# Router, row turning and clears of a conv/GLA + mixture-of-experts step rebuilt, one wait moved, fillers dropped

## The chip, the cores and the metric

One NeuronCore of a Trainium2 chip runs the whole program. The metric is the device time of one launch in microseconds; lower is better. The engines are TensorE (PE, products; PEld its weight loads), VectorE (DVE), ScalarE (ACT), GpSimd (POOL) and SyncE (SP, which only issues the loads).

## The reference

320 tokens (256 of a prompt, 64 of a running stream) of width 1024 go through two layers in fp32:

```python
for l in range(2):
    m = mixer(x, ...)                    # short gated convolution and gated linear attention, one in and one out projection
    x = layer_norm(ALPHA * x + m)
    if l == 0: f = (silu(x @ w_gate) * (x @ w_up)) @ w_down          # 1024 -> 3584 -> 1024
    else:
        logits = x @ router                                          # 8 experts
        top_v, top_i = top_k(logits, 2); gates = softmax(top_v)
        f = sum over the token's two experts of gate * swiglu_e(x)
    x = layer_norm(ALPHA * x + f)
```

## The kernel before

**Layout.** x lies transposed in SBUF: 8 column blocks of 128 model columns by 320 tokens (x[:, k, :]). Each fp32 product with weights is made of three fast ones: both operands are split into a rounded part and a rest (xh, xl; whi, wlo), and hi*hi, lo*hi and hi*lo are added up in PSUM. Weights arrive in units of 1 MB in a ring of six (raw); ACT rounds a unit (round_unit), DVE forms its rest (rest_unit), both two units ahead of PE (ring of three). SP loads unit n when the rest of unit n-6 exists (load). Units 0 to 15 are layer 0's mixer, 16 to 57 the dense mixer (7 chunks of 6), 58 to 73 layer 1's mixer, from 74 the experts. Every engine runs its program in the order written; semaphores tie them together.

**A norm** (norm on each engine) runs over the model columns, thus over partitions. DVE adds each new x[k] into rstd and each of ACT's squares into sq_sum while the blocks come; PE multiplies the sums by a matrix of 1/1024 (mean_d) and so spreads mean and mean square over all partitions (ps[4], ps[5]). DVE forms the variance (L1417, L1420), ACT Ln and Exp (L1096, L1098), DVE centres (L1423) and scales (L1441) each block; ACT adds the bias. Where the norm is split (behind layer 0's mixer and behind the dense mixer), ACT writes xh (L1102), DVE writes xl (L1432) and POOL adds the bias to x itself (add_bias, L550). PE fills its waits with products that nobody reads (keep_busy, L642; the counts stand in BUSY).

**The end of the dense mixer** (dense_mixer, last chunk): PE's unit 57 gives x[4] to x[7]; DVE adds each block to x (L1673), then into the sums; ACT rounds units 58 and 59, loads the table set for Ln and Exp (L1230) and then squares (L1088). DVE's rest of unit 59 stands behind its last addition. PE waits for the fourth addition and then does 8 fillers.

**Layer 1's mixer** begins with two_tiles over unit 58 block by block as xl comes, then 16 low-rank products (L792, L793) behind a wait for all of POOL's x, then unit 59.

**The router** stands behind layer 1's first norm, whose last step on ACT is x itself (L1107). PE multiplies x[k], as the weights loaded, by the 8 router columns, for three tiles of tokens (t): 24 fp32 products (L876), each two instructions. Then 24 transposes turn x into rows of tokens (L885), in six halves (512 columns each) in XT_ORDER. ACT rounds each half (xt_hi, L1247), DVE forms its rest (xt_lo, L1709). DVE clears lg, does rest_unit(76) and six memsets (clear), copies the logits (L1730) and ranks them (L1736 to L1743), marks first and second (sel1, sel2, sel) and forms the difference for the gates; each such small operation waits for the one before (step). PE counts places in each expert's list (L891 to L895), does 14 fillers and then four gathers (L914): the products of the turned rows with a 0/1 matrix (pick, L1832), which put the tokens of the first two experts side by side. ACT and DVE split what comes (xg). Before the first two gathers ACT must have kept two turned halves (kept, L1240), which frees their banks.

**The experts.** A pair of experts takes 84 units; pair() steps through gate and up units, transposes of the hidden rows (T, L977) and down units. In the first pair DVE also does the tables of the routing. hm is silu(gate)*up (L1901).

Of the kernel before, what the change touches and what calls it, by code (L numbers as in the profile page):

```python
# [33 lines left out]
def hybrid_stream_step(nc, x_prompt, x_sample, cache_conv, state_gla, ln_mix_g, ln_mix_b, w_in, w_alpha2,  # L34
# [86 lines left out]
    with ctx:  # L121
# [13 lines left out]
        mean_v = sb("mean_v", [P, P])  # L135
# [13 lines left out]
        w_rt = sb("w_rt", [P, KT, E])  # L149
# [255 lines left out]
        def _(sp):  # L405
# [16 lines left out]
            def parameters():  # L422
# [14 lines left out]
                sp.dma_start(w_rt[:], moe_router[0].rearrange("(k p) e -> p k e", p=P)).then_inc(small_landed, 16)  # L437
# [65 lines left out]
        def _(pool):  # L503
# [13 lines left out]
            const(pool.memset(mean_v[:], 1.0 / DV))  # L517
# [88 lines left out]
        def _(pe):  # L606
# [1409 lines left out]
```

## Time and profile before

| | us |
|---|---|
| median of 3 runs (lowest, highest) | 1613.78 (1612.58, 1614.01) |
| the profiled execution's own time | 1612.82 |
| its span | 1611.2 |
| PE busy | 1584.7 (98%) |
| DVE busy | 1248.0 (77%) |
| ACT busy | 1023.9 (64%) |
| POOL busy | 36.2 (2%) |
| granted TensorE clock, mean | 0.993 |

The span runs from the first to the last instruction that the profile holds; the time of a run is a little longer. A busy share is an average over stages with different limits. An fp32 product is two instructions of PE in the profile, an fp32 transpose one, and their ends are modelled, so distances between starts say more than durations. A granted clock of 1 is 2.4 GHz, of 0.5 it is 1.2 GHz.

### The profile page before, as it was taken

Reading aid. Unit: us, or ns where it says so; the run is one execution under the profiler, and the core shown is the slowest. Engines: PE = TensorE matmul, PEld = TensorE weight load, DVE = VectorE, ACT = ScalarE, POOL = GpSimd, SP = SyncE. Lnnn points to the kernel's source line nnn. Section 1 sums busy time; section 2 is a strip of 40 time slices with the busy share of each in tenths; the row PEclk is TensorE's granted clock in tenths of the full one; section 3 lists DMA queues with packets and bytes.
Section 4 is the critical chain, followed back from the end, with each engine's and each line's share of the span. In section 5 each row is a group of like instructions: output and inputs, shape, how many; then the busy total and the mean of one; then the engine's idle time right before and its main releaser. Section 6 shows DMA issues by size and latency. Waiting matters only on the chain.

```text
span 1611.2 us, 23720 instructions
## 1 busy us (share of the span) xinstructions
PE 1584.7 (98%) x8698; PEld 1405.7 (87%) x8698; DVE 1248.0 (77%) x1420; ACT 1023.9 (64%) x1178; POOL 36.2 (2%) x67
## 2 busy tenths in 40 slices
PE   9999999999989999999999999999999999999997
PEld 8998999999989998888888888888888888888885
DVE  5577554544475677999998998988898988898996
ACT  4454333333344555878777877877877877877875
POOL 1002000000010000000000000000000001000100
PEclk9999999999999998999999999999999999999999
DMA  9524644444424342999998999998999999999992
GB/s 300 165 79 161 214 155 156 143 143 156 144 92 131 106 138 102 364 374 372 383 380 330 383 370 380 385 370 324 381 371 375 384 377 351 385 395 378 387 394 80
DMA packets 226208, 445.41 MB, mean 276 GB/s; under 512 B 10498, under 2 KB 72656, under 8 KB 226064
## 3 DMA queue, kind: packets, MB, share of 16 engines
q1 hardware_dynamic: 223920, 434.16, 74.9%
q0 software_dynamic: 2192, 9.98, 1.7%
q8 instruction: 59, 0.97, 0.2%
q14 instruction: 37, 0.30, 0.1%
HBM read 438.59 MB, written 8.67 MB: 278 GB/s over the span
## 4 chain that ended last, share of the span: by engine, by line
PE 93%; DVE 4%; ACT 1%; issue 1%; DMA 0%; DVEq 0%; ACTq 0%
PE ps L964 18%; PE ps L939 13%; PE ps L941 13%; PE ps L940 13%; PE ps L610 10%; PE ps L611 10%; PE ps L612 10%; PE ps L977 1%; PE ps L914 1%; DVE x L1441 1%; DVE x L1423 1%; PE ps L642 0%; DVE wlo L1356 0%; DVE xl L1432 0%; PE ps L1009 0%
## 5 line engine op out<-in xcount | busy, mean ns | idle before, releaser
L1356 DVE TENSOR_TENSOR wlo<-raw,whi 128x1024 fp32r<-128x1024 f32 x672 | 778.2, 1218 | 48.8 <-ACT whi L1063 47.5
L1063 ACT ACTIVATE whi<-raw 128x1024 fp32r<-128x1024 f32 x672 | 677.3, 1055 | 59.7 <-PE ps L964 54.1
L939 PE MATMUL ps<-whi,xg 128*128 128x512 f32 x896 | 353.9, 395 | 0.0
L941 PE MATMUL ps<-whi,xg 128*128 128x512 f32 x896 | 349.5, 390 | 0.0
L940 PE MATMUL ps<-wlo,xg 128*128 128x512 f32 x896 | 348.9, 389 | 0.0
L1351 DVE TENSOR_TENSOR wlo<-raw,whi 128x2048 fp32r<-128x2048 f32 x73 | 167.5, 2294 | 128.2 <-ACT whi L1059 128.2
L610 PE MATMUL ps<-xh,whi 128*128 128x320 f32 x832 | 259.8, 312 | 4.7 <-DVE xl L1432 4.4
L612 PE MATMUL ps<-xh,wlo 128*128 128x320 f32 x832 | 257.1, 309 | 0.0
L611 PE MATMUL ps<-xl,whi 128*128 128x320 f32 x832 | 257.0, 309 | 0.0
L941 PEld LDWEIGHTS ps<-whi,xg 128*128 128x128 f32 x896 | 168.2, 188 | 35.8
L940 PEld LDWEIGHTS ps<-wlo,xg 128*128 128x128 f32 x896 | 168.4, 188 | 33.6
L939 PEld LDWEIGHTS ps<-whi,xg 128*128 128x128 f32 x896 | 168.3, 188 | 33.4
L1059 ACT ACTIVATE whi<-raw 128x2048 fp32r<-128x2048 f32 x73 | 139.1, 1906 | 62.9 <-PE ps L612 60.4
L610 PEld LDWEIGHTS ps<-xh,whi 128*128 128x128 f32 x832 | 156.1, 188 | 9.2 <-issue 4.5
L611 PEld LDWEIGHTS ps<-xl,whi 128*128 128x128 f32 x832 | 156.2, 188 | 0.2
L612 PEld LDWEIGHTS ps<-xh,wlo 128*128 128x128 f32 x832 | 156.2, 188 | 0.0
L964 PE MATMUL ps<-whi,hT_hi 128*128 128x512 f32 x440 | 135.6, 389 | 0.0
L964 PE MATMUL ps<-wlo,hT_hi 128*128 128x512 f32 x440 | 135.5, 389 | 0.0
L964 PE MATMUL ps<-whi,hT_lo 128*128 128x512 f32 x440 | 135.5, 389 | 0.0
L1305 ACT ACTIVATE hT_hi<-ps 128x512 fp32r<-128x512 f32 x56 | 33.6, 599 | 101.4 <-PE ps L977 101.0
L964 PEld LDWEIGHTS ps<-whi,hT_lo 128*128 128x128 f32 x440 | 82.6, 188 | 17.2
L964 PEld LDWEIGHTS ps<-wlo,hT_hi 128*128 128x128 f32 x440 | 82.6, 188 | 17.2
(322 smaller groups left out, 1506.4 us busy)
## 6 DMA issues: line engine op xcount, KB each, us to landing
raw<-in_moe_w_gate SPq DMA_DIRECT2D x112, 1024.0 KB, 8.1
raw<-in_moe_w_up SPq DMA_DIRECT2D x112, 1024.0 KB, 8.2
raw<-in_moe_w_down SPq DMA_DIRECT2D x112, 1024.0 KB, 7.6
raw<-in_w_in SPq DMA_DIRECT2D x23, 1024.0 KB, 5.5
raw<-in_ffn_w_gate SPq DMA_DIRECT2D x14, 1024.0 KB, 5.0
raw<-in_ffn_w_up SPq DMA_DIRECT2D x14, 1024.0 KB, 5.0
raw<-in_ffn_w_down SPq DMA_DIRECT2D x14, 1024.0 KB, 5.0
raw<-in_w_out SPq DMA_DIRECT2D x8, 1024.0 KB, 5.2
```

Of the source, the lines that this page charges most:

```text
L610: pe.matmul(out, wh, hi, start=start and j == 0, stop=False)
L611: pe.matmul(out, wh, lo, start=False, stop=False)
L612: mm = pe.matmul(out, wl, hi, start=False, stop=stop and j == len(pairs) - 1)
L939: pe.matmul(bank[:], xh_k, wh, start=k == 0, stop=False)
L940: pe.matmul(bank[:], xh_k, wl, start=False, stop=False)
L941: mm = pe.matmul(bank[:], xl_k, wh, start=False, stop=k == KT - 1)
L964: mm = pe.matmul(ps[4 + d][:], hT[:, c % 2, k, :], slot(w, n, SPLIT, 2)[:, j, 512 * d:512 * d + 512], start=fc == 0 and k == 0 and hT is h ...
L1059: act.activation(flat(whi, n, SPLIT), flat(raw, n, RAW), ACT.Copy).then_inc(hi_ready, 2)
L1063: act.activation(part(whi, n, SPLIT, h), part(raw, n, RAW, h), ACT.Copy).then_inc(hi_ready, 1)
L1305: act.activation(hT_hi[:, c % 2, :, :].rearrange("p f s -> p (f s)"), bank[:], ACT.Copy).then_inc(hT_hi_ready, 1)
L1351: dve.tensor_tensor(flat(wlo, n, SPLIT), flat(raw, n, RAW), flat(whi, n, SPLIT).bitcast(F32), ALU.subtract).then_inc(lo_ready, 2)
L1356: dve.tensor_tensor(part(wlo, n, SPLIT, h), part(raw, n, RAW, h), part(whi, n, SPLIT, h).bitcast(F32), ALU.subtract).then_inc(lo_ready, 1)
```

## The change

1. **Logits.** The router weights get 120 zero columns behind them (w_wide), a slice of 128 columns from 8k on is the loaded operand, and x[:, k, :] (320 columns) moves: 8 products into ps[0], of whose rows the first 8 are read. DVE copies them (lgT), PE turns them with three small transposes, DVE copies the result into lg. Behind these transposes PE does 9 fillers, and 5 instead of 14 ahead of the first gather.
2. **Turned rows.** The three transposes of block k follow the logit product of block k (the last two blocks behind all logits). XT_ORDER is now the first halves of all three token tiles, then the second halves, in other banks; ACT rounds the first three halves inside the norm, between its last blocks of x. The first two gathers wait for the first three rests alone.
3. **Selection.** sel is one comparison (rank below 2) and one memset. sel1, sel2, the gates' difference and the table copy stand behind the four gathers on DVE, and ACT's Exp of the difference behind its last kept half. The first pick reads qpos itself.
4. **Clears.** Five memsets go to POOL, which waits for the last unit of layer 1's mixer, and PE waits for them before the gathers; gT is cleared only in its last 64 columns. acc_sum stays with DVE.
5. **Units.** rest_unit(76) goes to the end of DVE's router. Unit 59 is rounded on ACT behind the Exp of the norm behind the dense mixer and its rest is formed behind that norm on DVE. The table load stands behind the fourth square.
6. **Waits and fillers.** In layer 1 PE no longer waits for POOL's x ahead of the low-rank products; DVE waits for it, block by block, where it updates x at the mixer's end. The 8 fillers behind the dense mixer are dropped.
7. mean_v (1/128) is dropped: the products use ones, and ACT's Ln gets the scale 1/128.

```diff
@@ -146,7 +145,8 @@
         w_a2 = sb("w_a2", [LRC, DEPTH, HEADS * DK])
-        w_rt = sb("w_rt", [P, KT, E])
+        w_wide = sb("w_wide", [P, KT * E + P - E])
+        w_rt = w_wide[:, 0:KT * E].rearrange("p (k e) -> p k e", e=E)
         u_mem = sb("u_mem", [P, CT * (T + 2 * (CONV_W - 1))])
@@ -371,9 +373,10 @@
-        BUSY = {"x lands": 5, "x tile": 2, "first unit": 5, "norm": 19, "last chunk": 8, "first gather": 14}
-        RT_LOGITS, RT_SEL, RT_DIFF = 4, 14, 19
-        XT_ORDER = [1, 2, 3, 4, 5, 0]
+        BUSY = {"x lands": 5, "x tile": 2, "first unit": 5, "norm": 19, "logits": 9, "first gather": 5}
+        RT_LOGITS, RT_SEL, RT_DIFF = 2, 11, 23
+        XT_ORDER = [0, 2, 4, 1, 3, 5]
+        XT_BANK = {0: 6, 2: 7, 4: 3, 1: 4, 3: 5, 5: 2}
         SMALL_LOADS = 4
@@ -571,6 +574,13 @@
         add_bias(1, o_ffn_b, 1.0)
+pool.wait_ge(unit_used, 2 * (U_OUT[1] + UNITS_OUT))
+for n, rows_of in enumerate((xt_hi[TOK[2]:P, 2, :].bitcast(F32), xt_lo[TOK[2]:P, 2, :].bitcast(F32),
+                             acc[TOK[2]:P, 2, :], gT_hi[:, T:TT * P].bitcast(F32),
+                             gT_lo[:, T:TT * P].bitcast(F32))):
+    if n:
+        pool.wait_ge(cleared, n)
+    pool.memset(rows_of, 0.0).then_inc(cleared, 1)
 pool.wait_ge(y_parked, 16)
...
     idle = ps[0 if stage == 3 else 7]
-    if stage == 1:
-        pe.wait_ge(d_added, 8 * FC + KT // 2)
-        keep_busy(BUSY["last chunk"], idle)
     pe.wait_ge(summed, (KT - 1) * (stage + 1))
@@ -783,8 +790,8 @@
-    pe.wait_ge(x_ready, KT * (1 + 2 * l))
     if l == 0:
+        pe.wait_ge(x_ready, KT)
         pe.wait_ge(small_landed, 16 * SMALL_LOADS)
@@ -869,22 +876,28 @@
+def turn_rows(k):
+    for t in range(TT):
+        mm = pe.transpose(ps[XT_BANK[2 * t + k // 4]][0:TOK[t], P * (k % 4):P * (k % 4) + P],
+                          x[:, k, P * t:P * t + TOK[t]], ident[:])
+        if k % 4 == 3:
+            mm.then_inc(xt_done, 1)
+
 def router():
...
         pe.wait_ge(x_ready, 3 * KT + k + 1)
-        for t in range(TT):
-            mm = pe.matmul(ps[t][0:TOK[t], 0:E], x[:, k, P * t:P * t + TOK[t]],
-                           w_rt[:, k, :], start=k == 0, stop=k == KT - 1)
+        mm = pe.matmul(ps[0][:, 0:T], w_wide[:, E * k:E * k + P], x[:, k, :], start=k == 0, stop=k == KT - 1)
+        if k < KT - 2:
+            turn_rows(k)
     mm.then_inc(lg_done, 1)
-
-    for j in XT_ORDER:
-        t, half = j // 2, j % 2
-        if j == 0:
-            pe.wait_ge(rt_step, RT_LOGITS)
-        for k in range(4):
-            mm = pe.transpose(ps[2 + j][0:TOK[t], P * k:P * k + P],
-                              x[:, 4 * half + k, P * t:P * t + TOK[t]], ident[:])
-        mm.then_inc(xt_done, 1)
+    turn_rows(KT - 2)
+    turn_rows(KT - 1)
+
+    pe.wait_ge(rt_step, RT_LOGITS)
+    for t in range(TT):
+        mm = pe.transpose(ps[1][0:TOK[t], E * t:E * t + E], lgT[:, P * t:P * t + TOK[t]], ident[0:E, 0:E])
+    mm.then_inc(lg_turned, 1)
+    keep_busy(BUSY["logits"], ps[0])
@@ -896,9 +909,10 @@
     keep_busy(BUSY["first gather"], ps[0])
-    pe.wait_ge(xtl_ready, 2 * TT)
+    pe.wait_ge(cleared, 5)
     pe.wait_ge(pick_ready, 1)
     for g in range(GATHERS):
+        pe.wait_ge(xtl_ready, TT if g < 2 else 2 * TT)
         if g < 2:
@@ -1081,6 +1095,13 @@
+def turned_hi(n):
+    j = XT_ORDER[n]
+    t, half = j // 2, j % 2
+    act.wait_ge(xt_done, n + 1)
+    act.activation(xt_hi[0:TOK[t], t, 512 * half:512 * half + 512], ps[XT_BANK[j]][0:TOK[t], :], ACT.Copy
+                   ).then_inc(xth_ready, 1)
+
 def square(stage, k):
...
     act.activation(rstd[:], rstd[:], ACT.Exp, scale=-0.5).then_inc(rstd_ready, 1)
+    if stage == 1:
+        round_unit(U_IN[1] + 1)
     if split:
...
                        ).then_inc(x_ready, 1)
+        if k >= KT - TT:
+            turned_hi(k - (KT - TT))
@@ -1226,38 +1252,36 @@
         chunk(c)
-    chunk(FC - 1)
-    act.preload_act_table_set(LOG_EXP)
+    chunk(FC - 1, last=True)
     for k in range(KT):
...
         square(1, k)
+        if k == 3:
+            act.preload_act_table_set(LOG_EXP)
     norm(1, o_ffn_b, True)
...
 def router():
-    def kept(j):
+    def kept(n):
+        j = XT_ORDER[n]
         t, half = j // 2, j % 2
-        act.wait_ge(xtl_ready, XT_ORDER.index(j) + 1)
-        act.activation(acc[0:TOK[t], t, 512 * half:512 * half + 512], ps[2 + j][0:TOK[t], :], ACT.Copy,
+        act.wait_ge(xtl_ready, n + 1)
+        act.activation(acc[0:TOK[t], t, 512 * half:512 * half + 512], ps[XT_BANK[j]][0:TOK[t], :], ACT.Copy,
                        scale=ALPHA).then_inc(acc_ready, 1)
...
+    for n in range(TT, 2 * TT):
+        turned_hi(n)
     round_unit(U_MOE + AHEAD)
-    for n, j in enumerate(XT_ORDER):
-        t, half = j // 2, j % 2
-        act.wait_ge(xt_done, n + 1)
-        act.activation(xt_hi[0:TOK[t], t, 512 * half:512 * half + 512], ps[2 + j][0:TOK[t], :],
-                       ACT.Copy).then_inc(xth_ready, 1)
-    act.wait_ge(rt_step, RT_DIFF)
-    act.activation(top[:, 3, :], top[:, 2, :], ACT.Exp).then_inc(rt_exp, 1)
-
-    kept(4)
-    kept(5)
+    kept(0)
+    kept(1)
     for g in range(GATHERS):
...
         if g == 1:
-            kept(1)
-    for j in (2, 3, 0):
-        kept(j)
+            kept(2)
+    for n in range(3, 2 * TT):
+        kept(n)
+    act.wait_ge(rt_step, RT_DIFF)
+    act.activation(top[:, 3, :], top[:, 2, :], ACT.Exp).then_inc(rt_exp, 1)
     act.preload_act_table(ACT.Silu)
@@ -1631,6 +1655,8 @@
                 dve.wait_ge(tile_done, TD_OUT[l] + u + 1)
+            if l:
+                dve.wait_ge(x_ready, 2 * KT + m + 1)
             dve.scalar_tensor_tensor(out=x[:, m, :], in0=x[:, m, :], scalar=ALPHA, in1=ps[m % 4][:, 0:T],
@@ -1677,24 +1703,13 @@
                             add_to_squares(1, k - 1)
-        if last:
-            rest_unit(U_IN[1] + 1)
...
     norm(1, o_ffn_g, o_ffn_b, True)
-
-def clear():
-    dve.wait_ge(unit_used, 2 * (U_OUT[1] + UNITS_OUT))
-
-    dve.memset(xt_hi[TOK[2]:P, 2, :].bitcast(F32), 0.0)
-    dve.memset(xt_lo[TOK[2]:P, 2, :].bitcast(F32), 0.0)
-    dve.memset(acc[TOK[2]:P, 2, :], 0.0)
-    dve.memset(acc_sum[:], 0.0)
-    dve.memset(gT_hi[:].bitcast(F32), 0.0)
-    dve.memset(gT_lo[:].bitcast(F32), 0.0).then_inc(m_hid, 1)
+    rest_unit(U_IN[1] + 1)
@@ -1722,13 +1737,14 @@
     dve.wait_ge(stored, 16 * LAYER_STORES * DEPTH)
+    dve.memset(acc_sum[:], 0.0).then_inc(m_hid, 1)
     step(dve.memset(lg[:], 0.0))
-    rest_unit(U_MOE + AHEAD)
-    clear()
     dve.wait_ge(lg_done, 1)
-    for t in range(TT):
-        step(dve.tensor_copy(lg[0:TOK[t], t, :], ps[t][0:TOK[t], 0:E]))
+    step(dve.tensor_copy(lgT, ps[0][0:E, 0:T]))
     assert n == RT_LOGITS
+    dve.wait_ge(lg_turned, 1)
+    step(dve.tensor_copy(lg[:, 0:2, :], ps[1][:, 0:2 * E].rearrange("p (t e) -> p t e", e=E)))
+    step(dve.tensor_copy(lg[0:TOK[2], 2, :], ps[1][0:TOK[2], 2 * E:3 * E]))
@@ -1741,28 +1757,31 @@
     step(dve.tensor_reduce(rank[:], cmp_gt[:], AXX, ALU.add))
+    step(dve.tensor_scalar(sel[:], rank[:], 2.0, None, ALU.is_lt))
+    dve.memset(sel[TOK[2]:P, 2, :], 0.0).then_inc(rt_step, 1)
+    n += 1
+    assert n == RT_SEL
+
+    xt_rest(0, TT)
+    dve.wait_ge(pos_done, 1)
+    step(dve.scalar_tensor_tensor(out=qpos[:], in0=ps[1][:, 0:TT * E].rearrange("p (t e) -> p t e", e=E),
+                                  scalar=1.0, in1=sel[:], op0=ALU.add, op1=ALU.mult))
+    make_pick(0, qpos)
+    xt_rest(TT, 2 * TT)
+    step(dve.tensor_copy(over_n[:, 0:E], ps[1][:, TT * E:TT * E + E]))
+    for g in range(GATHERS):
+        read_gather(g)
+    step(dve.tensor_copy(q_tab[:, :, 0:STATIC], qpos[:, :, 0:STATIC]))
     step(dve.tensor_scalar(sel1[:], rank[:], 0.0, None, ALU.is_equal))
...
     step(dve.memset(sel2[TOK[2]:P, 2, :], 0.0))
-    step(dve.tensor_tensor(sel[:], sel1[:], sel2[:], ALU.add))
-    assert n == RT_SEL
-
-    for m, s in enumerate((sel1, sel2)):
-        step(dve.tensor_tensor(tmp_e[:], s[:], lg[:], ALU.mult))
+    for m, sel_m in enumerate((sel1, sel2)):
+        step(dve.tensor_tensor(tmp_e[:], sel_m[:], lg[:], ALU.mult))
         step(dve.tensor_reduce(top[:, m, :], tmp_e[:], AXX, ALU.add))
...
     assert n == RT_DIFF
-    xt_rest(0, 4)
-    dve.wait_ge(pos_done, 1)
-    step(dve.scalar_tensor_tensor(out=qpos[:], in0=ps[1][:, 0:TT * E].rearrange("p (t e) -> p t e", e=E),
-                                  scalar=1.0, in1=sel[:], op0=ALU.add, op1=ALU.mult))
-    step(dve.tensor_copy(q_tab[:, :, 0:STATIC], qpos[:, :, 0:STATIC]))
-    make_pick(0)
-    xt_rest(4, 2 * TT)
-    step(dve.tensor_copy(over_n[:, 0:E], ps[1][:, TT * E:TT * E + E]))
-    for g in range(GATHERS):
-        read_gather(g)
+    rest_unit(U_MOE + AHEAD)
     return step
```

## Rows read from the trace of the kernel before

**Rows 1.** The page, chain of work that ended last, shares of the span by engine.
```profile
PE 93%; DVE 4%; ACT 1%; issue 1%; DMA 0%; DVEq 0%; ACTq 0%
```

**Rows 2.** Timeline, PE, end of the dense mixer (start, us, engine, line, operation, count).
```profile
448.51 1.95 PE L642 MATMUL ps<-mean_d 128*128 128x128 f32 x16
```

**Rows 3.** Timeline, DVE, same stretch (in brackets: idle before it, and its releaser).
```profile
445.48 0.33 DVE L1412 COPY u_mem<-u_mem 128x320 f32<-128x320 f32 x1 [3.90 <-ACT u_mem L1088]
...
452.35 0.48 DVE L1673 TENSOR_TENSOR x<-x,ps 128x320 f32<-128x320 f32 x1
...
455.47 0.48 DVE L1417 SCALAR_TENSOR_TENSOR u_mem<-u_mem,ps 128x320 f32<-128x320 f32 x1
```

**Rows 4.** Timeline, ACT, same stretch.
```profile
441.75 1.91 ACT L1059 ACTIVATE whi<-raw 128x2048 fp32r<-128x2048 f32 x1 [4.25 <-PE ps L612]
```

**Rows 5.** Busy time by stretch: width, PE, PEld, DVE, ACT, POOL, granted clock, DMA share, GB/s.
```profile
600.90:611.30 10.40, 10.40 (x51) 9.71 (x52) 7.98 (x17) 6.23 (x10) 0.00 (x0) 0.51 0.31 101
...
614.50:621.40 6.90, 6.90 (x35) 6.90 (x35) 5.33 (x13) 1.39 (x3) 0.00 (x0) 0.52 0.01 4
```

**Rows 6.** Timeline, DVE, router.
```profile
604.00 2.36 DVE L1356 TENSOR_TENSOR wlo<-raw,whi 128x1024 fp32r<-128x1024 f32 x2 [1.61 <-ACT whi L1063]
...
610.53 0.50 DVE L1730 COPY lg<-ps 128x8 f32<-128x8 f32 x3
...
613.02 0.18 DVE L1744 TENSOR_SCALAR sel<-rank 128x24 f32<-128x24 f32 x1
...
614.97 2.48 DVE L1709 TENSOR_TENSOR xt_lo<-ps,xt_hi 128x512 fp32r<-128x512 f32 x4
...
617.78 0.96 DVE L1832 TENSOR_TENSOR pick<-slot_no,q_tab 128x768 fp32r<-128x768 f32 x1
```

**Rows 7.** Timeline, PE, router.
```profile
598.59 1.68 PE L876 MATMUL ps<-w_rt,x 128*128 128x8 f32 x13
...
606.82 5.02 PE L885 MATMUL ps<-ident,x 128*128 128x128 f32 x24
...
613.94 0.40 PE L891 MATMUL ps<-sel,before 128*128 128x24 f32 x2 [2.10 <-DVE sel L1748]
...
615.81 6.11 PE L642 MATMUL ps<-mean_d 128*128 128x128 f32 x28
...
621.68 0.61 PE L914 MATMUL ps<-pick,xt_hi 128*128 128x256 f32 x3
...
627.82 0.40 PE L939 MATMUL ps<-whi,xg 128*128 128x512 f32 x1
```

**Rows 8.** Timeline, DVE and PE, the norm of layer 1.
```profile
592.08 0.49 DVE L1634 SCALAR_TENSOR_TENSOR x<-x,ps 128x320 f32<-128x320 f32 x1 [1.38 <-PE ps L612]
...
593.27 0.70 PE L687 MATMUL ps<-u_mem,mean_d 128*128 128x320 f32 x2
...
593.81 0.70 PE L689 MATMUL ps<-u_mem,mean_d 128*128 128x320 f32 x2
...
594.60 0.49 DVE L1417 SCALAR_TENSOR_TENSOR u_mem<-u_mem,ps 128x320 f32<-128x320 f32 x1 [1.50 <-PE ps L689]
```

**Rows 9.** Timeline, PE, first and last of 16 spacings, low-rank products of layer 1.
```profile
469.77 0.31 PE L792 MATMUL ps<-xh,w_split 128*128 128x320 f32 x1
...
472.11 0.31 PE L610 MATMUL ps<-xh,whi 128*128 128x320 f32 x1
```

**Rows 10.** Timeline, ACT, last blocks of x.
```profile
601.00 1.95 ACT L1107 ACTIVATE x<-x,prm 128x320 f32<-128x320 f32 x4 [0.30 <-DVE x L1441]
```

**Rows 11.** A line's instructions, ns min/median/max; and POOL's timeline at the start.
```profile
L1432 DVE SCALAR_TENSOR_TENSOR xl<-x,prm,xh x16: 536/542/819, 150.1 to 467.3; 128x320 fp32r<-128x320 f32 x16
...
6.49 0.52 POOL L543 MEMSET v_tok<- 64x512 f32 x1
```

**Rows 12.** Timeline, DVE and PE, first pair of experts.
```profile
639.62 0.68 DVE L1901 TENSOR_TENSOR hm<-sg,ps 128x512 f32<-128x512 f32 x1
...
641.45 0.60 PE L977 MATMUL ps<-ident,hm 128*128 128x128 f32 x4
```

More of the change, by code:

```diff
@@ L134, in hybrid_stream_step @@
         mean_d = sb("mean_d", [P, P])
-        mean_v = sb("mean_v", [P, P])
         ones = sb("ones", [P, P])
@@ L295, in hybrid_stream_step @@
         gb_rows = x[:, :, :].rearrange("p k t -> p (k t)")[:, 0:2 * D].rearrange("p (a d) -> p a d", a=2)
+        lgT = hm[0:E, 0, 0:T]
         y_park = nc.dram_tensor("y_park", [SLOTS * P, D], F32).ap()
@@ L331, in hybrid_stream_step @@
         d_silu, d_hid, d_hh, d_hl, d_added = (sem(n) for n in ("d_silu", "d_hid", "d_hh", "d_hl", "d_added"))
+        lg_turned, cleared = sem("lg_turned"), sem("cleared")
         lg_done, xt_done, xth_ready, xtl_ready, rt_step, rt_exp, pos_done, ctl_ready = (sem(n) for n in (
@@ L436, in parameters @@
                                  ).then_inc(small_landed, 16)
-                sp.dma_start(w_rt[:], moe_router[0].rearrange("(k p) e -> p k e", p=P)).then_inc(small_landed, 16)
+                sp.dma_start(w_rt, moe_router[0].rearrange("(k p) e -> p k e", p=P)).then_inc(small_landed, 16)
             def given_states():
@@ L516, in _ @@
             const(pool.memset(mean_d[:], 1.0 / D))
-            const(pool.memset(mean_v[:], 1.0 / DV))
+            const(pool.memset(w_wide[:, KT * E:], 0.0))
             const(pool.memset(ones[:], 1.0))
@@ L777, in mean_squares @@
                         pe.wait_ge(o_sq[l], h + 1)
-                        pe.matmul(ps[4 + h][:, 0:T], mean_v[:], proj[:, h, :], start=True, stop=True
+                        pe.matmul(ps[4 + h][:, 0:T], ones[:], proj[:, h, :], start=True, stop=True
                                   ).then_inc(ms_done[l], 1)
@@ L1160, in rms @@
                         act.wait_ge(ms_done[l], h + 1)
-                        act.activation(proj[:, TV + h, :], ps[4 + h][:, 0:T], ACT.Ln, bias=cst[:, 0:1]
+                        act.activation(proj[:, TV + h, :], ps[4 + h][:, 0:T], ACT.Ln, bias=cst[:, 0:1], scale=1.0 / DV
                                        ).then_inc(ms_act[l], 1)
@@ L1208, in dense_mixer, with chunk @@
             def dense_mixer():
-                def chunk(c):
+                def chunk(c, last=False):
                     for j in range(PER_CHUNK):
-                        round_unit(U_FFN + j + AHEAD, c, PER_CHUNK)
+                        if not last or j < 5:
+                            round_unit(U_FFN + j + AHEAD, c, PER_CHUNK)
                         q = j // 2
@@ L1708, in xt_rest @@
                         cols = slice(512 * half, 512 * half + 512)
-                        dve.tensor_tensor(xt_lo[0:TOK[t], t, cols], ps[2 + j][0:TOK[t], :],
+                        dve.tensor_tensor(xt_lo[0:TOK[t], t, cols], ps[XT_BANK[j]][0:TOK[t], :],
                                           xt_hi[0:TOK[t], t, cols].bitcast(F32), ALU.subtract).then_inc(xtl_ready, 1)
@@ L1826, in lo_of_pair, with make_pick @@
                                   xg[:, 2 * g:2 * g + 2, 0, :].bitcast(F32), ALU.subtract).then_inc(job_read, 1)
-            def make_pick(i):
+            def make_pick(i, tab=q_tab):
                 at = slice(2 * i, 2 * i + 2) if isinstance(i, int) else bass.ds(i * 2, 2)
@@ L1832, in make_pick @@
                 dve.tensor_tensor(pick[:], slot_no[:].unsqueeze(1).unsqueeze(1).to_broadcast(full),
-                                  q_tab[:, :, at].unsqueeze(3).to_broadcast(full), ALU.is_equal).then_inc(pick_ready, 1)
+                                  tab[:, :, at].unsqueeze(3).to_broadcast(full), ALU.is_equal).then_inc(pick_ready, 1)
             def rows_of_tokens(c, step):
```

## The prediction

> **What bounds the kernel now.** I read the chain that ended last first: TensorE (PE) holds 93% of it [rows 1]. An engine full of products gains only where its products are not the limit, so I looked next for stretches in which it sits idle, runs at half clock or multiplies fillers. The change touches two of them: the norm behind the dense mixer (about 440 to 461 us) and the router (about 595 to 628 us).
>
> In the first, the last product of the dense mixer is issued just ahead of 448.51, where eight fillers follow it at once [rows 2]; yet VectorE (DVE) adds the last column block x[7] only at 452.35 [rows 3]. The reason stands in its timeline: it waited 3.90 us, to 445.48, for the first square [rows 3], and ScalarE (ACT) was late with it because it rounded a unit of weights that is not needed yet (1.91 us, from 441.75, itself held up by PE) and then loaded a table [rows 4].
>
> In the router PE looks 100% busy, and isn't. Its granted clock is 0.51 from 600.9 to 611.3 and 0.52 from 614.5 to 621.4 [rows 5]: 1.2 in place of 2.4 GHz. What it did before the first fall was logits with 8 moving columns; before the second it was idle 2.10 us. DVE holds the sum of the waits: it forms the logits' ranks only from 610.53, because the weight rest of 604.00 (2.36 us) and six memsets stand ahead of them [rows 6]. Behind the selection PE does 14 fillers, 615.81 to 621.68, though the pick is there at 617.78 + 0.96 = 618.74 [rows 6, 7].
>
> **The norm behind the dense mixer.** With the weight unit (U_IN[1]+1) moved behind the norm on both engines and the table load behind the fourth square, ACT is free when x[0] is added. DVE then needs 1.33 us for one block (445.48 to 452.35 holds a short copy and five of them [rows 3]) and PE gives a block in 12 products of 0.146, 1.76 us (16 stand between 469.77 and 472.11 [rows 9]), so PE sets the pace. x[7] follows the last product: in the next norm DVE's last addition is 592.08, 0.20 behind PE's next instruction, so 448.51 + 0.20 = 448.71 in place of 452.35: **-3.64 us**. From there to the variance the next norm, with nothing between, takes 592.08 to 594.60 = 2.52; this one took 452.35 to 455.47 = 3.12, since the weight rest stood between [rows 3, 8]: **-0.60**. ACT now rounds that unit (1.91) between the exponential and the first rounded x. The first rounded x comes later by part of that, but DVE asks for it only after three scalings and six centrings, which begin with the exponential: I take 0, with 0.9 as the other end, what would be left after two of DVE's 0.5 us operations. The removed eight fillers cover nothing any more, for PE is idle only some tenths between its last product and the mean. Price 0. What is late next: the moved rest (2.3 to 2.5 us) now ends behind the last rest of x. PE has the last third of a block and the 16 low-rank products (2.34 us [rows 9]) to do before it needs it; slack about 1.4. Its raw buffer is freed later and so the load of the unit six further on goes out about 11 us later; PE comes to that one six units of 48 products, 42 us, on. The wait for x that PE loses had no idle in front of it, since GpSimd adds its bias right behind each rest; at its reader, DVE's update of x at the end of the mixer, it is long satisfied: 0. Sum here: **-4.2**.
>
> **Router, step by step.** (a) Logits. PE starts at 598.59 as before [rows 7]. One logit product with 320 moving columns costs what the norm's sums cost at full clock, 593.27 to 593.81 = 0.54 [rows 8]; a transpose costs 5.02/24 = 0.21 at half clock [rows 5, 7], so about 0.105 at full. Six blocks of 0.54 + 3 x 0.105 = 0.86 end at 603.7; the last two products start at 603.7 and 604.3. ACT delivers the last four x by 602.95 (four in 1.95) [rows 10]; two of the three roundings of turned rows now stand ahead of the last x, 0.5 each, so it comes at 603.95: PE is the later by a little. A product is read 0.79 behind its start (593.81 to 594.60) [rows 8]: logits are readable at 605.1. Before, 610.53.
> (b) New: a copy of 8 x 320 out of PSUM. The copy of 128 x 320 in SBUF is 0.33 [rows 3], the rest of 128 x 512 out of PSUM is 2.48/4 = 0.62 [rows 6]; I take 0.4, nearer the row of the same width. Then three small transposes with their hand-over (0.6), and two copies at 0.17 (three take 0.50 [rows 6]): 606.5.
> (c) Ranks: 610.53 to 613.02 less the three copies is 2.0, as before; then one comparison and one memset (0.35) in place of five steps (0.92, 613.02 to 613.94): selection ready at 608.8. Before, 613.94 [rows 6, 7].
> (d) Whole rows: DVE takes three rests of xt (2.48/4 = 0.61 each) instead of four, then position (0.2) and pick (0.96) without the table copy: pick ready at 608.8 + 1.83 + 0.2 + 0.96 = **611.8**. PE's position products (1.3 at full clock, 2.1 if slow) and five fillers (1.1) end at 611.2 under it. The first gathers need only half 0 of all rows, and that is there. First gather at 611.9, before 621.68: **-9.8 us**.
> From there the four gathers run as before (6.14 us to the first gate product), as the three late rests of xt end at 613.7, just before the first gather can be read.
>
> **GpSimd's clears.** 64 x 512 costs 0.52 [rows 11], so three of 64 x 1024 and two of 128 x 64 cost about 3.4 us. They start behind its last stores of layer 1, beside the norm's scaling, and are wanted at 611.9. Price in itself 0. But they run beside DVE's eight operations of the norm. While GpSimd added biases, DVE's fused operation rose from 0.54 to at most 0.82 [rows 11]; eight times 0.15 is 1.2, ends 0 and 1.2. x has 0.3 in hand and PE's fillers run 0.5 over the first x, so I take **+0.3**, nearer the free end. The Trainium skill, SBUF — State Buffer, in "SBUF: two separate sides", says a DVE operation with two SBUF inputs clashes only with a GpSimd operation that reads SBUF; a memset reads nothing, and by that the term would be 0 and the sum 0.3 better.
>
> **What is queued late.** The rest of unit 76 (2.36) and 11 small steps (1.9) now stand behind the last gather on DVE, and ACT's exponential waits for those steps. With G the first gate product (627.82 before [rows 7]): steps end at G + 3.4, the rest of 76 at G + 5.8, its first half at G + 4.6; PE wants it at G + 5.5. ACT (exponential, table, one copy) starts unit 77 at G + 5.2, DVE has its first half at G + 7.5; wanted at G + 8.2. Then DVE carries the backlog: the product hm ends at G + 14.1, where it ended at G + 12.5, and PE's first transpose of it stood at G + 13.6 [rows 12]: **+0.5**. In later chunks that transpose stands behind more products. SP's load of unit 82 is released 17 us later, at G + 5.8, but it is wanted only when unit 79 is used up, about G + 17.
> The ones matrix with a scale of 1/128 in the activation, the wider router weights and one memset for another at the start change nothing on the path.
>
> **Sum.** -4.2 - 9.8 + 0.3 + 0.5 = -13.2 us. Against the profiled execution's own 1612.82 (span 1611.2) that is 1599.6; the median shown is 1.0 above it, 1613.78, so I forecast 1600.5. A measurement of this kernel can tell about 0.2%, 3.2 us, from no change.
>
> **Rivals.** *The clock falls all the same* (chance 0.2). For: between the lgT transposes and the first gather PE has pauses of some 0.6 us, small products and only 14 fillers. Against: the long stretch of 8-column products and the 2.10 us of idle are gone. In the rows it stayed at half for 6.9 us; put over positions and gathers that costs 3.4: 1603.9. The Trainium skill, TensorE: Matmul & The Clock Gate, in "Part 1: The HAM clock gate", holds that low recent activity gates the clock; the trace agrees with its 0.51, and by that rule dropping fillers is what speaks against this change.
> *The late rests hold up the first pair* (0.06). All slacks there are 0.7 to 1 us; if ACT and DVE slip by 3 us more, PE waits 3: 1603.5. Were the weight stream the limit, one lost load in advance costs the same 2.8 us.
> *The gain is taken back* (0.03): the change moves the start of the expert stage, but that stage ends by something else. Against: every load is released by DVE's rests, so the stream moves with the start. It would leave the 4.2 at most or nothing: 1610 to 1614.
> *Slower* (0.03): the gathers wait for GpSimd's five clears. DVE and GpSimd could lock each other out, each memset waiting for a gap. It decides only when the fifth ends past 611.9 + 13.2 = 625.1, that is 5.6 us a memset instead of 0.9. At 7 us each it gives 1620. Nothing in the rows is near that.
>
> **Numbers.** The forecast has 0.68 with its own range 1599 to 1602 (GpSimd 0 to 1.2, copy, hm 0 to 0.6, the rounding 0 to 0.9). The range reaches over the clock's fall and below for a better hand-over: 1597.5 to 1604.5. Faster 0.94, same 0.03, slower 0.03.
>
> **What would show it.** Right: x[7] added at about 448.7 and DVE's variance at 451.2; first product on the next weights 4.2 earlier; granted clock 1.00 from 590 through the logits; ranks begun near 602.3 (606.5 less 4.2), first gather near 607.9. Wrong: idle in front of the second input unit; a clock near 0.5 at the gathers; a wait for GpSimd's memset; idle of PE at the third or fourth unit of the first pair above 1 us.

## The result, and the profile of the changed kernel

Slower, where I had forecast 13 us faster: 1622.92 us (median of 4 runs, 1622.23 to 1623.11) against 1613.69 for the kernel before; ratio 1.006, 95% interval 1.0048 to 1.0072. The profiled execution took 1623.11, span 1621.5.

First the stretches that the change was made for. Timelines of the changed kernel, DVE and PE: the end of the dense mixer, the logits, the ranks, the first gather and the first gate product.
```profile
449.46 0.31 PE L622 MATMUL ps<-hh,wlo 128*128 128x320 f32 x1
...
449.80 0.49 DVE L1699 TENSOR_TENSOR x<-x,ps 128x320 f32<-128x320 f32 x1 [0.27 <-PE ps L622]
...
452.33 0.49 DVE L1441 SCALAR_TENSOR_TENSOR u_mem<-u_mem,ps 128x320 f32<-128x320 f32 x1 [1.51 <-PE ps L696]
...
602.01 0.48 DVE L1743 COPY hm<-ps 8x320 f32<-8x320 f32 x1 [2.74 <-PE ps L889]
...
603.36 0.36 DVE L1752 TENSOR_TENSOR cmp_gt<-lg 128x192 f32<-128x192 f32 x1
...
607.66 0.96 DVE L1851 TENSOR_TENSOR pick<-slot_no,qpos 128x768 fp32r<-128x768 f32 x1
...
608.72 0.59 PE L928 MATMUL ps<-pick,xt_hi 128*128 128x256 f32 x3 [0.32 <-issue]
...
614.89 0.40 PE L953 MATMUL ps<-whi,xg 128*128 128x512 f32 x1
```
The kernel before has that last product of the dense mixer at 448.36, just ahead of its fillers:
```profile
448.36 0.31 PE L612 MATMUL ps<-hh,wlo 128*128 128x320 f32 x1
```
It is 1.10 later here, a difference of the run's first microseconds (over all the traces, of either kernel, it scatters from 447.67 to 449.58). With it taken off, every date is the forecast one within 0.1: x[7] added at 448.70 (forecast 448.71), variance 451.23 (451.23), logits read at 600.9 (605.1 less 4.2), ranks begun 602.26 (602.3), first gather 607.6 (611.9 less 4.2). The granted clock stays up, where [rows 5] had 0.51 and 0.52 (busy time by stretch, columns as in [rows 5]):
```profile
600.00:610.00 10.00, 9.07 (x69) 7.89 (x68) 7.15 (x18) 6.00 (x10) 0.00 (x0) 1.00 0.00 0
```
The first gate product stands at 614.89, before at 627.82 [rows 7]: 12.93 us earlier, 14.03 with the start taken off. So the loss comes behind it. From the first gate product to the end of the span it took 983.4 before (1611.2 - 627.82) and 1006.6 now (1621.5 - 614.89), 23.2 more. PE waits there for 1.3 us in all in the kernel before and for 1.0 us now, so the loss is not idle time. Groups of instructions of PE, kernel before, then the changed one (busy us, mean ns | idle):
```profile
L939 PE MATMUL ps<-whi,xg 128*128 128x512 f32 x896 | 353.9, 395 | 0.0
L941 PE MATMUL ps<-whi,xg 128*128 128x512 f32 x896 | 349.5, 390 | 0.0
...
L610 PE MATMUL ps<-xh,whi 128*128 128x320 f32 x832 | 259.8, 312 | 4.7 <-DVE xl L1432 4.4 <-DVE wlo L1376 0.2
...
L964 PE MATMUL ps<-whi,hT_hi 128*128 128x512 f32 x440 | 135.6, 389 | 0.0
```
```profile
L953 PE MATMUL ps<-whi,xg 128*128 128x512 f32 x896 | 358.4, 400 | 0.0
L955 PE MATMUL ps<-whi,xg 128*128 128x512 f32 x896 | 353.8, 395 | 0.0
...
L620 PE MATMUL ps<-xh,whi 128*128 128x320 f32 x832 | 260.4, 313 | 3.9 <-DVE xl L1456 3.8
...
L978 PE MATMUL ps<-whi,hT_hi 128*128 128x512 f32 x440 | 138.3, 395 | 0.0
```
Every product with 512 moving columns is 5 to 6 ns longer; those with 320 columns are not. The same in a quiet stretch far from the change, kernel before, then the changed one: 11 products fewer in 100 us at the same clock of 1.00 and nearly the same DMA traffic (last two columns: share and GB/s).
```profile
900.00:1000.00 100.00, 100.00 (x454) 82.75 (x453) 88.98 (x83) 77.98 (x85) 0.00 (x0) 1.00 1.02 377
```
```profile
900.00:1000.00 100.00, 100.00 (x443) 80.66 (x443) 87.45 (x83) 76.66 (x84) 0.53 (x1) 1.00 1.01 369
```
The chain that ended last gives the spacing, for 24 products with the hidden rows, before and then now: 5.44 / 24 = 0.2267 and 5.60 / 24 = 0.2333 us.
```profile
650.26 5.44 PE ps L964 x24
```
```profile
637.88 5.60 PE ps L978 x24
```

The experts have 3 x 896 + 3 x 440 = 4008 such products in these groups; 23.2 us over 4008 is 5.8 ns each. That is the whole loss behind the first gate product.

### The profile page after: what moved, and what is told of

Its sections match the earlier page's. It is cut to its first block, busy times and chain, and to the rows that moved or that the text cites. A ratio compares the mean times of both kernels' runs of the same rounds, so it can differ in the third digit from the quotient of the medians.

```text
span 1621.5 us, 23644 instructions
## 1 busy us (share of the span) xinstructions
PE 1599.2 (99%) x8653; PEld 1395.3 (86%) x8653; DVE 1246.3 (77%) x1416; ACT 1022.5 (63%) x1178; POOL 43.3 (3%) x72
## 4 chain that ended last, share of the span: by engine, by line
PE 96%; DVE 3%; issue 1%; ACT 0%; DVEq 0%; POOL 0%; ACTq 0%; POOLq 0%
PE ps L978 19%; PE ps L953 13%; PE ps L955 13%; PE ps L954 13%; PE ps L620 11%; PE ps L622 11%; PE ps L621 11%; PE ps L928 1%; PE ps L991 1%; PE ps L652 1%; DVE x L1465 1%; DVE xl L1456 0%; DVE x L1447 0%; PE ps L1023 0%; PE ps L770 0%
## 5 line engine op out<-in xcount | busy, mean ns | idle before, releaser
L953 PE MATMUL ps<-whi,xg 128*128 128x512 f32 x896 | 358.4, 400 | 0.0
L955 PE MATMUL ps<-whi,xg 128*128 128x512 f32 x896 | 353.8, 395 | 0.0
L954 PE MATMUL ps<-wlo,xg 128*128 128x512 f32 x896 | 353.7, 395 | 0.0
```

The source lines that it names most:

```text
L953: pe.matmul(bank[:], xh_k, wh, start=k == 0, stop=False)
L954: pe.matmul(bank[:], xh_k, wl, start=False, stop=False)
L955: mm = pe.matmul(bank[:], xl_k, wh, start=False, stop=k == KT - 1)
```

## The experiments

Nothing in the experts' code was changed. But item 7 of the change drops mean_v (512 bytes a partition) and the wider router weights add 480, and both stand ahead of most tiles in SBUF. Added up in order of allocation, every tile behind them begins 32 bytes lower: xg, hT_hi, hT_lo and pick, but not whi and wlo, which stand ahead. The experiments take this apart. In this table a tile's start is given in bytes behind a multiple of 256; all slices of these tiles that PE reads lie whole multiples of 256 further on. The last column is the time from the first gate product to the end of the span.

| kernel | whi, wlo | xg | hT | time, us | experts, us |
|---|---|---|---|---|---|
| before | 128 | 128 | 128 | 1613.69 | 983.4 |
| changed | 128 | 96 | 96 | 1622.92 | 1006.6 |
| e1, changed, pad 32 | 128 | 128 | 128 | 1600.77 | 983.7 |
| e2, before, pad 32 | 128 | 160 | 160 | 1637.01 | 1007.0 |
| e3, changed, pad behind xg | 128 | 96 | 128 | 1614.79 | 998.0 |
| e5, changed, pad ahead of the weights | 160 | 128 | 128 | 1624.31 | 1006.6 |
| e4, changed, pad 96 | 128 | 192 | 192 | 1624.11 | 1007.5 |
| e6, changed, all 32 on | 160 | 160 | 160 | 1599.66 | 983.3 |

**e1: the changed kernel with its tiles put back.**
```diff
         w_rt = w_wide[:, 0:KT * E].rearrange("p (k e) -> p k e", e=E)
+        sb("pad", [P, 8])
```


> The changed kernel with 32 unused bytes per partition behind the router weights, so that every tile behind them lies where it lay before the change. Theory A (addresses: without mean_v and with the wider router weights all later tiles lie 32 bytes lower, and the products of the expert stage, whose loaded operands xg and hT no longer start at a multiple of 64 bytes, are spaced 0.2333 us instead of 0.2271): spacing back to 0.2271, 4032 products x 0.0062 = 25 us less, 1598 us. Rival B (the late rests of the router leave VectorE or ScalarE behind through the expert stage): nothing changes, 1623. Rival C (a slower run of this program by chance, of clock or memory): 1623 as well or anything between.

1600.77 us (1599.88 to 1601.66, 4 runs), ratio to before 0.9921, interval 0.9905 to 0.9938. Eight floats that nobody reads are worth 22 us, and the kernel then stands where the prediction had it. That rules out both rivals, a lag of VectorE or ScalarE (B) and mere chance (C). Its group of gate products:
```profile
L954 PE MATMUL ps<-whi,xg 128*128 128x512 f32 x896 | 353.9, 395 | 0.0
```

**e2: the same pad in the kernel before.**
```diff
         w_rt = sb("w_rt", [P, KT, E])
+        sb("pad", [P, 8])
```


> The kernel before with 32 unused bytes behind the router weights and nothing else: all later tiles 32 bytes higher. Theory A: expert products spaced 0.2333 instead of 0.2271, 1613.7 + 25 = 1638.7 us. Rival B and C: 1613.7.

1637.01 us, ratio 1.0149 (1.0132 to 1.0166): 23.4 us slower by the pad alone, with nothing of the change in it. The layout is enough in both directions. By the table's last column the experts take 23.6 us more.

**e3: pad behind xg only.**
```diff
         sbl("xg_rest", [P, KT * 4 * P - 2 * D])
+        sbl("pad", [P, 8])
```


> The changed kernel with 32 unused bytes between xg and the tiles behind it: xg stays at 32 modulo 64, hT_hi, hT_lo and pick are at 0. Theory A (it is the loaded operand of each product): gate and up products (xg loaded) keep a mean of 395 to 400 ns, down products (hT loaded) go back from 395 to 389 ns; 1344 x 0.0062 = 8.3 us less, 1614.6 us. Another theory D (any tile misplaced in the stage slows all of it, as through VectorE's and ScalarE's accesses): both groups move together.

1614.79 us (one run). The cost goes with the tile, product by product: those with xg stay long, those with hT are short again, so it is no slowness of the whole stage (theory D).
```profile
L954 PE MATMUL ps<-whi,xg 128*128 128x512 f32 x896 | 358.4, 400 | 0.0
...
L979 PE MATMUL ps<-whi,hT_hi 128*128 128x512 f32 x440 | 135.6, 389 | 0.0
```
In these products xg and hT are the loaded operand (128 columns) and the weights whi, wlo move (512 columns).

**e5: pad ahead of the weights, xg and hT back in place.**
```diff
+        sb("pad", [P, 8])
         raw = sb("raw", [P, RAW * UNIT])
```


> The changed kernel with 32 unused bytes ahead of everything: raw, whi, wlo, x, the identity and the ones matrices at 32 modulo 64, all tiles behind the router weights at 0. Theory A (loaded operand): the expert stage (xg, hT loaded at 0, whi moving at 32) is back at 0.2271; in the dense mixers whi and wlo are the loaded operand and now at 32: their spacing of 0.1467 would rise by about 0.006 for 3328 products, so 1598 + 20 = 1618 us. Against A stands that the low-rank products of the kernel before loaded w_split from an address of 32 modulo 64 and kept 0.146: if a load from there costs only beside 512 moving columns, the dense stages stay at 0.1467 and the time is 1598. Theory E (the two operands must lie alike modulo 64): the expert stage stays slow, 1623, and the dense stages too may slow.

1624.31 us (one run), gate products again at 400 ns. The loaded operand lay where the kernel before has it, so a rule for the loaded operand alone (theory A in its first form) falls. What stays is that the two must lie alike (theory E), or that each has its own rule.

**e6: weights and loaded operands moved together.**
```diff
+        sb("pad", [P, 8])
         raw = sb("raw", [P, RAW * UNIT])
...
+        sbl("pad_late", [P, 8])
         pair_s = ExitStack()
```


> The kernel after, with pads so that weights (whi, wlo) and the experts' operands (xg, hT) all lie 32 bytes from a multiple of 64. Theory E (they must lie alike): products of the experts spaced 0.227 us again, about 1601. Theory A (each must begin at a multiple of 64): 0.233 or more, 1623 or above.

1599.66 us (one run); the products are spaced as before. Theory A in both forms falls: every operand is 32 bytes off, and it costs nothing, since all are off alike.

**e4: 96 bytes ahead of xg.**
```diff
+        sbl("pad", [P, 24])
         pair_s = ExitStack()
```


> The kernel after with 96 bytes ahead of xg: xg and hT at a multiple of 64 but not of 128, weights at a multiple of 128. If 64 bytes is what counts: about 1601, as with the pad of 32 bytes. If 128: about 1624, as without a pad.

1624.11 us (one run). A distance of 64 bytes costs as much as one of 32: alike modulo 64 is not enough.

**e7 and e12: the price by itself.** Behind the last output of the kernel before, 60 fillers and then groups of 36 products with nothing beside them. Each group stands in the program with its own numbers; here it is written once, with w and m for the starts of the weights and of the moving operand in floats and n for the columns. The tiles themselves begin alike.
```diff
             combine()
+            pe.wait_ge(y_ready, 2 * TT)
+            keep_busy(60)
+            for j in range(36):
+                pe.matmul(ps[7][:, 0:n], wlo[:, w + P * (j % 8):w + P * (j % 8) + P],
+                          whi[:, m + 512 * (j % 8):m + 512 * (j % 8) + n], start=True, stop=True)
```


> The kernel before with a probe behind its last output: 60 fillers, then 17 groups of 36 fp32r products, each with the weights (128 columns of wlo) and the moving operand (columns of whi) begun so many bytes from a multiple of 64, nothing else running. Both theories: 512 columns with both at 0 are spaced 0.227 us. Theory E (loaded and moving operand must lie alike modulo 64 bytes): 0.227 for 0/0, 32/32 and 16/16, 0.233 for 32/0, 0/32, 16/0, 0/16 and 32/16. Theory A (each must begin at a multiple of 64): 0.233 for everything but 0/0, 64/0 and 0/64. A third (the cost needs DVE's and ACT's traffic beside it): all groups 0.227. 64/0 and 0/64 are 0.227 if the modulus is 64, 0.233 if it is 128. 320 columns 0.147 with either offset, as in the dense stages; 256, 384 and 448 say from which width it costs.

> The probe again, 18 groups of 36 products, with other pairs (weights' start / moving operand's start in bytes behind a multiple of 128). Theory E in the form that the first probe left (alike modulo 128 bytes): with 512 columns 0.2275 for 0/128, 32/160, 64/64, 96/96 and 0/256, 0.233 for 0/96 and 32/0; 8/8 says whether the slight cost of 16/16 (0.230) grows below 32 bytes. Rival (only a start below both, 0/0 or 32/32, is free, and any longer distance costs): 0.233 for 0/128, 32/160 and 0/256. Widths: 32/0 against 0/0 differs by 6 ns at 512 and, if the cost fades with the width, by less at 480 and 448 and by 0 at 416, 384 and below; if it is a step, by 6 ns at 448 too (0.2042 there with 32/0 in the first probe).

Timeline of PE in e7, first five groups: weights/moving at 0/0, 32/0, 0/32, 32/32 and 16/0 bytes, then the three groups with 320 columns at 0/0, 32/0 and 0/32.
```profile
1623.83 8.44 PE L1053 MATMUL ps<-whi,wlo 128*128 128x512 f32 x36
1632.11 8.56 PE L1055 MATMUL ps<-whi,wlo 128*128 128x512 f32 x36
1640.50 8.56 PE L1057 MATMUL ps<-whi,wlo 128*128 128x512 f32 x36
1648.90 8.35 PE L1059 MATMUL ps<-whi,wlo 128*128 128x512 f32 x36
1657.10 8.55 PE L1061 MATMUL ps<-whi,wlo 128*128 128x512 f32 x36
...
1707.29 5.44 PE L1073 MATMUL ps<-whi,wlo 128*128 128x320 f32 x36
1712.57 5.44 PE L1075 MATMUL ps<-whi,wlo 128*128 128x320 f32 x36
1717.85 5.44 PE L1077 MATMUL ps<-whi,wlo 128*128 128x320 f32 x36
```
From start to start, over 36: 0/0 0.2300 (one product of it took 85 ns more; its median of 389 ns is that of 32/32, and a second 0/0 group at the probe's end has 0.2272), 32/0 0.2331, 0/32 0.2333, 32/32 0.2278. With 320 columns all three are 0.1467. Neither VectorE nor DMA traffic is needed for it. Timeline of PE in e12, the first eight groups, in this order: 0/0, 0/128, 32/160, 64/64, 96/96, 0/256, 8/8 and 0/96.
```profile
1624.10 8.44 PE L1053 MATMUL ps<-whi,wlo 128*128 128x512 f32 x36
1632.38 8.55 PE L1055 MATMUL ps<-whi,wlo 128*128 128x512 f32 x36
1640.77 8.56 PE L1057 MATMUL ps<-whi,wlo 128*128 128x512 f32 x36
1649.17 8.37 PE L1059 MATMUL ps<-whi,wlo 128*128 128x512 f32 x36
1657.38 8.36 PE L1061 MATMUL ps<-whi,wlo 128*128 128x512 f32 x36
1665.57 8.37 PE L1063 MATMUL ps<-whi,wlo 128*128 128x512 f32 x36
1673.78 8.57 PE L1065 MATMUL ps<-whi,wlo 128*128 128x512 f32 x36
1682.18 8.57 PE L1067 MATMUL ps<-whi,wlo 128*128 128x512 f32 x36
```
All pairs with 512 columns from both probes:

| weights/moving, bytes | us a product |
|---|---|
| 32/32, 64/64, 96/96, 0/256, second 0/0 | 0.2272 to 0.2281 |
| 0/0 as the first group of either probe, with one long product | 0.2300 |
| 16/16 | 0.2300 |
| 8/8 | 0.2333 |
| 0/16 | 0.2317 |
| 32/0, 0/32, 16/0, 64/0, 0/64, 32/16, 0/96, 0/128, 32/160 | 0.2328 to 0.2336 |

My form of the theory (alike modulo 128) missed two of its own pairs, 0/128 and 32/160. What fits all is alike modulo 256 bytes (that it is 256 and no larger rests on one pair, 0/256; every pair 16 to 128 bytes apart cost something); a common offset was free where it was a multiple of 32, and cost a little at 16 and all at 8. By width, 0/0 against 32/0: 0.2169 and 0.2197 at 480 columns; 0.2061 and 0.2044 at 448; 0.1886 and 0.1900 at 416; 0.1739 and 0.1733 at 384. So the price is 6 ns at 512, half of that at 480, and at 448 and below nothing beyond what single groups scatter (up to 2 ns). That fits the dense stages, whose products move 320 columns: whi and wlo begin at 128 there and xh and xl, by the same shift, at 96 in the changed kernel, and their products cost what they did before. The gathers say nothing on it, since both of their operands, pick and the turned rows, moved by the same 32 bytes.

**e8: the norm behind the dense mixer alone, in the kernel before.** Unit 59 rounded behind the Exp and its rest formed behind the norm, table load behind the fourth square, 8 fillers dropped; everything else, the layout too, as before.
```diff
                 act.activation(rstd[:], rstd[:], ACT.Exp, scale=-0.5).then_inc(rstd_ready, 1)
+                if stage == 1:
+                    round_unit(U_IN[1] + 1)
...
-                    if last:
-                        rest_unit(U_IN[1] + 1)
...
                 norm(1, o_ffn_g, o_ffn_b, True)
+                rest_unit(U_IN[1] + 1)
```


> The kernel before (its layout kept) with the norm behind the dense mixer alone changed: unit 59 rounded and rested behind the norm, the table load behind the fourth square, the 8 fillers dropped. By my steps 4.2 us faster: 1609.4. If the start of the second input unit waits for the moved rest (idle in front of it), 1611 to 1613.

1615.32 us (11 runs), ratio 1.0012 (1.0003 to 1.0021): slower by 2.4, not faster by 4.2. Timelines of PE, POOL and DVE, and the busy time and clock behind the gap:
```profile
465.96 0.31 PE L612 MATMUL ps<-xh,wlo 128*128 128x320 f32 x1
469.62 0.64 PE L789 MATMUL ps<-xh,w_split 128*128 128x320 f32 x1 [3.35 <-POOL x L550]
```
```profile
463.40 6.16 POOL L550 TENSOR_SCALAR x<-x,prm 128x320 f32<-128x320 f32 x3 [0.43 <-DVE xl L1433]
```
```profile
464.43 4.73 DVE L1352 TENSOR_TENSOR wlo<-raw,whi 128x2048 fp32r<-128x2048 f32 x2
```
```profile
469.60:472.70 3.10, 3.08 (x11) 3.09 (x12) 0.00 (x0) 0.00 (x0) 0.00 (x0) 0.50 1.10 368
```
The gain is there: the first product on the next weights stands 8.13 behind the last dense product (457.06 - 448.93), before 12.36 (460.72 - 448.36), 4.2 won. But DVE now forms two rests one behind the other, and GpSimd's last three bias additions, 0.52 us each when alone, take 6.16, the last two of them beside these rests. PE waits for all of GpSimd's x ahead of its low-rank products, 3.35 us, and then runs 3.1 us at half clock, some 1.6 lost: 5.0 against the 4.2 won. From the last dense product to the variance of layer 1's first norm it is 147.10 (596.03 - 448.93), before 146.24 (594.60 - 448.36): 0.9 slower. The two profiled executions differ by 1.4 (1614.23 - 1612.82); the other 0.6 lies ahead of the change, in the start. Of the 2.4 between the medians 1.5 stays unexplained.

**e9: the same with the wait moved** (part 6 of the change).
```diff
-                pe.wait_ge(x_ready, KT * (1 + 2 * l))
                 if l == 0:
+                    pe.wait_ge(x_ready, KT)
...
+                        if l:
+                            dve.wait_ge(x_ready, 2 * KT + m + 1)
```


> The kernel of e8_before_norm_alone plus the change's sixth part: in layer 1 TensorE no longer waits for GpSimd's x ahead of the low-rank products, and VectorE waits for it at the mixer's end. Theory (GpSimd's last bias additions are held up by the two rests that VectorE now does one behind the other, and only that wait made it cost): no idle at 466 us, granted clock 1.00 from 460 to 480, the 4.2 us of the norm come out: 1608.7 against before's 1612.9. Rival (the moved rest itself comes too late for the unit): the idle stays, 1613 to 1615.

1608.45 us (6 runs), ratio 0.9969 (0.9956 to 0.9981). The low-rank products follow at once, though GpSimd is as slow as in e8:
```profile
466.60 0.31 PE L789 MATMUL ps<-xh,w_split 128*128 128x320 f32 x1
```
```profile
463.89 6.17 POOL L550 TENSOR_SCALAR x<-x,prm 128x320 f32<-128x320 f32 x3 [0.43 <-DVE xl L1433]
```
So the two parts are one. The kernel before has no idle in front of that wait; once the rest has been moved, it costs 5.1 us: from the last dense product to the variance of layer 1's first norm e9 takes 142.00 (591.43 - 449.43), e8 147.10. The medians are 6.9 apart (1615.32 - 1608.45), but e9's router, which this edit does not touch, is 1.6 shorter in its trace as well (25.45 from that variance to the first gather, in e8 and before 27.08).

**e10 and e11: the fillers of the router**, both on e1.
```diff
-        BUSY = {"x lands": 5, "x tile": 2, "first unit": 5, "norm": 19, "logits": 9, "first gather": 5}
+        BUSY = {"x lands": 5, "x tile": 2, "first unit": 5, "norm": 19, "logits": 11, "first gather": 6}
```
(e11: "logits": 0, "first gather": 0.)

> The kernel of e1_after_shift32 with 11 fillers behind the logits' transposes instead of 9 and 6 ahead of the first gather instead of 5. Theory (the clock fell in that run from 608.5 to 612 because TensorE had paused twice): the granted clock is 1.00 at the gathers, first gate product 6.2 us behind the first gather instead of 7.6, about 1599.3 (1.5 us faster, 0.991 of before). Rival (the fall has another cause): 1600.8 and a clock near 0.5 there.

> The kernel of e1_after_shift32 without the 9 fillers behind the logits' transposes and without the 5 ahead of the first gather. If idle lets the clock fall: 0.5 from the position products to behind the gathers, at least 3.4 us more than at full clock, so 1603 to 1605. If the fillers don't matter: 1600.8.

In e1's profiled execution the granted clock was 0.54 from 608.5 to 612.2, behind a pause of 0.62 and one of 0.32 us; the changed kernel's had the same pauses and 1.00.
```profile
608.50:612.20 3.70, 3.70 (x18) 3.70 (x19) 1.88 (x5) 0.60 (x1) 0.00 (x0) 0.54 0.00 0
```
Six traces have this router with 9 and 5 fillers. The clock fell in four of them, in e1, e3 and e5 about where the gathers begin and in e6 already at 606.0, behind the pause of 0.62 alone; in the changed kernel's and in e4's it stayed at 1.00. Busy time by stretch from the first gather on, e10, then e11:
```profile
607.00:613.50 6.50, 6.27 (x51) 5.93 (x50) 4.07 (x8) 2.27 (x4) 0.00 (x0) 1.00 0.01 4
```
```profile
607.00:613.00 6.00, 5.48 (x26) 5.51 (x27) 2.97 (x6) 0.60 (x1) 0.00 (x0) 0.50 0.00 1
```
e10: 1599.30 us (5 runs), ratio 0.9916 (0.9903 to 0.993); first gather 607.36, first gate product 613.55, 6.19 apart, in e1 7.61. e11: 1602.88 us (4 runs), ratio 0.9937 (0.9922 to 0.9952), just below the 1603 to 1605 expected; 8.48 apart, so the missing fillers cost 2.3 against the 6.17 of the changed kernel (614.89 - 608.72), and not 3.4. It has these pauses:
```profile
604.48 0.40 PE L905 MATMUL ps<-sel,before 128*128 128x24 f32 x2 [2.82 <-DVE sel L1762]
...
607.52 0.98 PE L929 MATMUL ps<-pick,xt_hi 128*128 128x256 f32 x3 [1.53 <-DVE pick L1852]
```
Of the versions with more than one run e10 is the fastest: 23.6 us faster than the change as made, 13.7 faster than before. Its margin over e1, 1.5 us, is about the size of the scatter of e1's own runs (1.8). What speaks for it is the clock: 1.00 in the trace, and a mean of 0.997 or 0.998 in all five runs, where e1's four have 0.995 or 0.996. But the changed kernel's four have 0.997 or 0.998 too, with e1's router and e1's fillers; so it is not shown that the added fillers are what kept the clock up.

## Why the prediction was wrong

**The step that failed** is the last sentence of the working: "The ones matrix with a scale of 1/128 in the activation, the wider router weights and one memset for another at the start change nothing on the path." I priced these edits as instructions and did not look at what they do to the addresses behind them. Their price is 23.2 us, 4008 products at 5.8 ns: the expert stage's loaded operands came to lie 32 bytes off the weights that move against them, and e1 and e2 give and take that price with 8 floats alone. No rival held it either. The one that ended slower was GpSimd's clears; they cost nothing, and the range of 1597.5 to 1604.5 was drawn around times of instructions only. The sign was wrong because 23.2 is more than the 14 that the rest brings.

**The norm behind the dense mixer, -4.2**: right, in the changed kernel and in e9 (-4.6 by medians, some of it the router's scatter; 4.24 by the first product on the next weights, 457.58 - 449.46 = 8.12 behind the last dense product, before 12.36). But I priced the removed wait for x apart, as 0, with the argument that GpSimd is right behind each rest. That argument was taken from a kernel in which only one rest followed. e8 shows what it misses: without the moved wait this part alone is slower, and the wait is worth 5.1. That the -4.2 held is luck in this respect: the change happened to contain both parts.

**The router, -9.8**: right step by step, as the dates above show; the copy of the logits (0.48, taken as 0.4) and the hand-overs came out within 0.1. **GpSimd's clears, +0.3**: mis-sized, it is 0. The memsets run from 593.65 to 597.04 and are wanted at 608.7; DVE's operations of the norm beside them keep their 0.48 and 0.54 us. The Trainium skill, SBUF — State Buffer, in "SBUF: two separate sides", had it so: a DVE instruction with two SBUF inputs does not contend with a GpSimd instruction that only writes SBUF, as a memset does. **Queued late, +0.5**: the first transpose of hm stands 14.01 behind the first gate product, before 13.63 [rows 12], so +0.4.

**The sum** -13.2 against -13.7 in e10, whose clock stays up; e1, whose clock fell in the profiled execution, has -12.9. **The rival of the clock** (0.2) therefore does occur, in e1, e3, e5 and e6, four of the six traces with this router, though not in the changed kernel's; 0.2 was low, and with my 3.4 us it was oversized: 7.61 - 6.17 = 1.4 is what it costs in e1, and 8.48 - 6.17 = 2.3 without any fillers (e11).

## What to carry to other kernels

An allocation is part of the kernel: when a tile is added, dropped or resized, list where the operands of the main products begin before and after, and keep each loaded and moving pair alike modulo 256 bytes, with a pad if need be; here it mattered with 480 and 512 moving columns. When thousands of products cost the same in two kernels but for 1 or 2%, compare the spacing of their starts in a quiet stretch first; it tells a change of rate from a stall. And a wait that is free today may be so only because of the order that the same change gives up: price each wait in the order that the change will leave.

## What the runs showed of the hardware that I had not expected

- A product with 128x128 fp32r weights and 512 moving columns takes 0.227 us from start to start when both operands begin alike modulo 256 bytes in their partition, at a multiple of 32, and 0.233 when not, at the same granted clock of 1.00, with other engines at work (e1, e2) or without (e7, e12). Which part of the chip makes it so stays open; other types and other shapes of weights were not tried.
- A tensor-scalar of GpSimd on 128x320 took 2.88 and 2.56 us beside DVE's subtractions of two SBUF tiles (2.28 and 2.53 in e8), 0.52 without them: in e8 each addition ends 0.3 to 0.4 behind the end of a subtraction. The Trainium skill, SBUF — State Buffer, in "SBUF: two separate sides", holds that the port pair which the two share is an exclusive lock for a whole instruction, held by whichever starts first; the rows of e8 agree in that the additions end only when a subtraction is over. Who came first they can't show: the first addition is recorded 0.28 ahead of the first subtraction (464.15 and 464.43) and yet ends behind it, and GpSimd's times in the profile are rough.
- The same two pauses of PE, 0.62 and 0.32 us, were followed by half clock in e1's profiled execution (0.54) and by full clock in the changed kernel's (1.00), as in e4's; what decides it stays open. In e11, with pauses of 2.82 and 1.53 us, the clock was 0.50 for 6 us.
